# A transformer-layer kernel: the front of the program gets a fourth conditioning buffer, later state loads and a deeper token pipeline

## What is computed

```
sh1, sc1, g1, sh2, sc2, g2 = split(silu(cond) @ ada_w + ada_b, 6)    # cond: c_ctx and c, two rows
h = rms_norm(x, norm1_g) * (1 + sc1) + sh1                          # x_sample gets a position table first
z = h @ w_in                                                        # 2816 columns
y_rwkv, s_new = rwkv7_bidir(z_shift, z_g, s0, p)                    # s0 = state_rwkv for latent tokens
y_conv = conformer_conv(z_conv, p)                                  # 31 taps per channel
```

## Time and profile before

| | |
|---|---|
| time of the kernel before, median of 3 runs | 1143.97 us (1143.56 to 1144.54) |
| the profiled execution: span from first to last instruction | 1138.3 us |
| what lies around the span, against the median | 5.7 us |
| PE busy | 890.6 us (78%) |
| DVE busy | 550.1 us (48%) |
| ACT busy | 300.0 us (26%) |
| GpSimd (POOL) busy | 45.3 us (4%) |

### The profile page before, as it was taken

How to read it: one execution, slowest core, us unless ns; L and a number is a source line. 1 busy time by engine, 2 the same in 40 slices (tenths; PEclk the granted TensorE clock), 3 DMA queues, 4 the chain that set the end, 5 groups by cost and what they waited for, 6 DMA issues and landing times.

```text
span 1138.3 us, 17266 instructions
## 1 busy us (share of the span) xinstructions
PE 890.6 (78%) x6827; PEld 540.6 (47%) x6827; DVE 550.1 (48%) x1112; ACT 300.0 (26%) x522; POOL 45.3 (4%) x50
## 2 busy tenths in 40 slices
PE   1599988999988796967958959693298897997764
PEld 0366544666665674756746624343233242442321
DVE  1426999855357767677651534436611021111116
ACT  2241000150654645475212252101011010110102
POOL 0000000000000000000000000001101011110010
PEclk9989999999988587685765979795599898998987
DMA  9843354111200202001044078320499999997952
GB/s 316 266 192 130 134 215 186 61 56 29 20 2 10 21 1 30 2 11 21 4 81 163 4 238 318 145 93 37 157 419 421 420 420 410 419 420 293 417 204 118
DMA packets 75246, 196.50 MB, mean 173 GB/s; under 512 B 42885, under 2 KB 45311, under 8 KB 60959
## 3 DMA queue, kind: packets, MB, share of 16 engines
q1 hardware_dynamic: 66192, 174.19, 41.7%
q0 software_dynamic: 5472, 10.53, 2.5%
q10 hardware_dynamic: 3503, 10.68, 2.5%
HBM read 182.45 MB, written 21.31 MB: 179 GB/s over the span
## 4 chain that ended last, share of the span: by engine, by line
PE 42%; DVE 18%; DMA 13%; ACT 6%; issue 4%; SPq 2%; DVEq 0%; ACTq 0%; POOLq 0%
PE bank L2222 8%; DMA arena<-in_expert_w_up 7%; PE bank L539 5%; PE bank L1554 5%; DVE arena L969 4%; PE bank L2244 3%; PE bank L1222 2%; ACT arena L845 2%; PE bank L1279 1%; DMA arena<-winv 1%; DMA arena<-table_positions 1%; PE bank L1209 1%; PE bank L1282 1%; PE bank L1308 1%; DVE arena L1118 1%
## 5 line engine op out<-in xcount | busy, mean ns | idle before, releaser
L539 PE MATMUL bank<-arena 128*128 128x320 f32 x704 | 205.0, 446 | 2.1 <-ACT arena L389 2.1
L539 PEld LDWEIGHTS bank<-arena 128*128 128x128 f32 x704 | 133.6, 194 | 74.5 <-issue 25.3
L2222 PE MATMUL bank<-arena 128*64 128x512 f32 (+2 forms) x496 | 124.0, 665 | 22.2 <-DMA arena<-in_expert_w_up 21.3
L969 DVE SCALAR_TENSOR_TENSOR arena<-arena 128x655 f32<-128x655 f32 x116 | 104.7, 903 | 4.5
L2222 PEld LDWEIGHTS bank<-arena 128*64 128x64 f32 (+2 forms) x496 | 44.3, 152 | 100.2 <-issue 98.9
L2302 DVE TENSOR_TENSOR arena<-arena,bank 128x256 f32<-128x256 f32 x16 | 6.8, 422 | 141.7 <-ACT arena L2276 141.7
L1554 PE MATMUL bank<-arena 128*128 128x512 f32 x160 | 71.6, 605 | 0.0
L2244 PE MATMUL bank<-arena 128*64 128x512 f32 (+2 forms) x248 | 58.8, 599 | 9.4 <-DVE arena L2305 9.4
L1554 PEld LDWEIGHTS bank<-arena 128*128 128x128 f32 x160 | 30.7, 194 | 37.7 <-issue 37.7
L1308 PE MATMUL bank<-arena 64*64 64x64 f32 x320 | 32.5, 259 | 14.0 <-DVE arena L1136 14.0
L1308 PEld LDWEIGHTS bank<-arena 64*64 64x64 f32 x320 | 27.2, 167 | 26.4 <-DVE arena L1136 21.1
(11 more groups left out here) (352 smaller groups left out, 1300.3 us busy)
## 6 DMA issues: line engine op xcount, KB each, us to landing
arena<-in_expert_w_gate SPq DMA_DIRECT2D x33, 1024.0 KB, 16.7
arena<-in_expert_w_up SPq DMA_DIRECT2D x33, 1024.0 KB, 22.7
arena<-in_expert_w_down SPq DMA_DIRECT2D x33, 1024.0 KB, 22.2
arena<-in_ada_w SPq DMA_DIRECT2D x12, 2048.0 KB, 8.7
arena<-in_w_in SPq DMA_DIRECT2D x22, 512.0 KB, 3.8
arena<-expert_rows SPq DMA_DIRECT2D x10, 512.0 KB, 7.3
arena<-in_x_sample SPq DMA_DIRECT2D x8, 512.0 KB, 6.4
arena<-in_w_out SPq DMA_DIRECT2D x1, 4096.0 KB, 15.1
```

What stands on the lines that cost most here:

```text
L539: mm = nc.tensor.matmul(psum[4 + 2 * (n % 2) + half][:, 0:HALF], wring[:, n % NWIN, k], hT[:, k, half * HALF:(half + 1) * HALF], start=(k ...
L969: chain(nc.vector.scalar_tensor_tensor(acc, src, w, acc, ALU.mult, ALU.add))
L2222: mm = nc.tensor.matmul(psum[2 + n % 2][r, :], xeT[:, n % 2, c, r], gu[:, :, c, :], start=(c == 0), stop=(c == KD - 1))
```

## The change

All of it is in the first stage, except for renamed semaphores and one moved step.

- **A fourth buffer** `adaw3` for block 3, laid over `zlora`, `xlora` and `ysum`, which are free then. Block 3 has no wait any more and is issued between `w_in` tiles 0 and 1. Blocks 4 and up use the three old buffers; blocks 4, 5 and 6 wait for one summed block fewer than before. The three memsets of `zlora`'s padding move behind the wait for block 3's join.
- **States.** The eight loads leave SP's list and are issued by GpSimd, after a wait for the sum of block 3. `init.0` moves: on PE from between z.1.1 and z.1.2 to before `ada.5`, on DVE from behind `xl.0` to behind `tap.1.2`.
- **silu** moves on ACT from before the first square to between the copies of tiles 3 and 4.
- **Rows turned last.** PE's three transposes of the rows move behind those of the token tiles, and with them the DVE copies of `condP`, `par`, `convw` and `oneminus`. Block 1 now also waits for the last of these copies.
- **Token tiles two deep.** The position of tile i + 2 is added between the two halves of `normed(i)`, and ACT's root and copy are split off (`deviation`, `turned`), so that tile i's copy runs one step later.

```diff
+        adaw3 = view(zbase + 3 * PAIRS * ZT, KD * 512)
+        def ada_buffer(m):
+            if m == NADA:
+                return NADA, adaw3, 16
+            b = m if m < NADA else (m - NADA - 1) % NADA
+            return b, adaw[:, b], 16 * (1 + (m - 1) // NADA if m > NADA else 1)
 def ada_load(m):
-            if m >= NADA:
-                sp.wait_ge(s_adamm, m - NADA + 1)
+            if m > NADA:
+                sp.wait_ge(s_adamm, (m - NADA) if m <= 2 * NADA else m - NADA + 1)
 def sp_front():
             for m in range(NADA):
                 ada_load(m)
-            for a in range(8):
-                sp.dma_start(SL[0:64, a] ..., ins["state_rwkv"] ...).then_inc(s_sl, 16)
             win_tile(0)
+            ada_load(3)
             win_tile(1)
-            ada_load(3)
             win_tile(2)
 def pool_front():
+            nc.gpsimd.wait_ge(s_adamm, 4)
+            for a in range(8):
+                nc.gpsimd.dma_start(SL[0:64, a] ..., ins["state_rwkv"] ...).then_inc(s_sl, 16)
 def act_front():
-            act.wait_ge(s_rows, ROWS_ALL)
-            nc.scalar.activation(crow[0:16, :], crow[0:16, :], ACT.Silu).then_inc(s_silu, 1)
             square_sum(0)
             for i in range(TILES):
                 if i + 1 < TILES:
                     square_sum(i + 1)
-                turned(i)                      # square_sum held the root too
+                deviation(i)
+                if i:
+                    turned(i - 1)
+            act.wait_ge(s_rows, ROWS_ALL)
+            nc.scalar.activation(crow[0:16, :], crow[0:16, :], ACT.Silu).then_inc(s_silu, 1)
+            turned(TILES - 1)
 def dve_front():
+            def normed(i):
+                x = xt[:, i]
+                dve.wait_ge(s_xstat, i + 1)
+                ... variance ..., s_var, i + 1)
+                if i + 2 < TILES:
+                    position(i + 2)
+                dve.wait_ge(s_std, i + 1)
+                ... reciprocal, scale ..., s_xn, i + 1)
+            position(1)
+            for i in range(TILES):
+                normed(i)
+                if i:
+                    turned(i - 1)
+            turned(TILES - 1)
             dve.wait_ge(s_rowsT, 1)
             ... condP, par, convw, oneminus ...
-            for z in [zrkv[:, j, :] for j in range(12)] + [zlora]:
+            for z in [zrkv[:, j, :] for j in range(12)]:
             dve.wait_ge(s_modT, 4)
+            for c in (0, TP + 1, ZT - 1):
+                chain(nc.vector.memset(zlora[:, c:c + 1], 0.0))
 ORDER
-    pe:  ... z.1.1 init.0 z.1.2 ... z.6.0 ada.5 ...      dve: ... xl.0 init.0 join.4 ... tap.1.2 join.5 ...
+    pe:  ... z.1.1 z.1.2 ... z.6.0 init.0 ada.5 ...      dve: ... xl.0 join.4 ... tap.1.2 init.0 join.5 ...
```

More of the change, by code:

```diff
@@ L228, in build @@
         s_const, s_rows, s_lora = sem("constants_landed"), sem("rows_landed"), sem("lora_landed")
-        s_adaw = [sem(f"ada_block_landed{b}") for b in range(NADA)]
+        s_adaw = [sem(f"ada_block_landed{b}") for b in range(NADA + 1)]
         s_adab = [sem(f"ada_bias_landed{b}") for b in range(2)]
@@ L372, in square_sum, with deviation, turned @@
                                s_xstat, i + 1)
+            def deviation(i):
                 act.wait_ge(s_var, i + 1)
                 nc.scalar.activation(small[:, 8 + i:9 + i], small[:, i:i + 1], ACT.Sqrt).then_inc(s_std, 1)
+            def turned(i):
+                act.wait_ge(s_xT, i + 1)
+                chain.announce(nc.scalar.activation(
+                    hT[:, 0:4, i * P:(i + 1) * P], psum[4 + 2 * (i % 2)][:, :].rearrange("p (k t) -> p k t", t=P),
+                    ACT.Copy), s_hTa, i + 1)
             square_sum(0)
@@ L445, in dve_front @@
             chain(nc.vector.tensor_scalar(oneminus[:, 0:26], par[:, 0:26], -1.0, 1.0, ALU.mult, ALU.add))
[L446 to L468, removed]
-            for z in [zrkv[:, j, :] for j in range(12)] + [zlora]:
+            chain.announce(nc.vector.tensor_scalar(oneminus[:, 26:34], par[:, PAR["ka"]:PAR["ka"] + 8], -1.0, 1.0,
+                                                   ALU.mult, ALU.add), s_condT, 2)
+            for z in [zrkv[:, j, :] for j in range(12)]:
                 for c in (0, TP + 1, ZT - 1):
@@ L501, in ada_block @@
             pe = nc.tensor
-            pe.wait_ge(s_adaw[m % NADA], 16 * (m // NADA + 1))
+            b, w, landed = ada_buffer(m)
+            pe.wait_ge(s_adaw[b], landed)
             if m >= 2:
                 pe.wait_ge(s_adatmp, m - 1)
-            w = adaw[:, m % NADA].rearrange("p (k n) -> p k n", k=KD)
+            w = w.rearrange("p (k n) -> p k n", k=KD)
             for k in range(KD):
@@ L938, in act_mix @@
                     chain.announce(nc.scalar.activation(SL[0:64, 4:8], psum[7][0:64, :].rearrange("p (a b) -> p a b", b=P),
-                                                      ACT.Copy), s_finc, 1)
+                                                      ACT.Copy), s_s0, 2)
         def dve_pads(chain):
@@ L1346, in pe_mix @@
                                                  ST[:, 0, a, :], ident)
-                    mm.then_inc(s_fin, 1)
+                    mm.then_inc(s_slT, 1)
         EXPERT = 3 * 2048
```

42 lines of the change are left out of this document (28 added, 14 removed), and 8 rows, old and new, of the table ORDER.

## The result

| | before | after |
|---|---|---|
| median in the same series of runs | 1139.11 us (7 runs, 1135.93 to 1144.54) | 1131.19 us (7 runs, 1126.06 to 1132.75) |
| ratio of the two | | 0.9908 (95% interval 0.9880 to 0.9936) |
| profiled execution: span | 1138.3 us | 1127.2 us |
| profiled execution: its own time | not on record | 1128.92 us |
| first matmul of block 3 | 56.51 us | 45.18 us |

The change makes the kernel faster by 0.92%, some 10.5 us by the ratio (interval 0.64 to 1.20%). The ratio is worked out from all executions and is not the quotient of the two medians: that is 0.9930, or 7.9 us, and lies inside the interval. The ratio foretold (1133.3 / 1143.97) was 0.9907.

The account below looks back on a forecast made before the run. Bound: one DVE list waiting for z.2, behind block 3's load. z.0 -10.7, z.2 -0.6 and DVE +0.7 made -10.7 us: span 1138.3 to 1127.6, with 5.7 around it 1133.3; range 1130.5 to 1138.5.

Parts of the forecast that it names:

- Bound before: Up to 222 us: DVE's list can't begin before z.2 is summed, so the front is worth what it moves z.2.
- Block 3's landing: DMA queue in the front: block 3's load lands at 44.8 us, bounds 43.0 and 47.3.
- the states' price in the queue: DMA ahead of block 3: the eight state loads cost 2.5 us, which lets w_in tile 0 land at 39.8.
- The estimate of 0.85 us: States' DMA cost from descriptor cycles: 0.85 us; block 3 would land at 46.4, the gain 1.6 us less.
- Landing to z.0: Block 3's landing to z.0: 8.24 us as before, memsets 0.37, lower clock 0.6; z.0 at 54.0, 10.7 earlier.
- the middle way: Rival, front: PE stays at the lower clock or loads share the engines; 2 to 4 us less gain, 1136.5; chance 0.20.
- The level: Whole kernel: span 1127.6 plus the 5.7 us around it gives 1133.3, the same as 1143.97 - 10.7.
- Tokens: Front: tokens only have to stay ahead of block 3; shortened by over 10 us, they yield nothing beyond 44.8.
- Slower by the clock: Rival, z.0 to z.2: sparser PE work keeps the clock at 0.50 through them; 1149 us, chance 0.05.
- GpSimd in DVE's way: Rival, modulation of hT: GpSimd's eight issues lock out DVE; z.0 loses up to 4.4 us; 1135, chance 0.07.
- Nothing gained: Rival: block 3's load doesn't run ahead, or DVE's earlier start meets something fixed in time; 1143 us, chance 0.09.
- the likeliest case: Whole kernel: the forecast itself, chance 0.52, with its own bounds of 1130.8 to 1136.5 us.

Follow-up runs that it names:

- pe_kept_busy: Changed kernel with six added 128 x 512 matmuls on PE, behind the joins of blocks 0, 1 and 3; ratio to the kernel before 0.9895.
- front_trimmed: Changed kernel with block 3 issued ahead of w_in tile 0, low-rank weights loaded later and three added matmuls; 1120.07 us, ratio to before 0.9817.
- no_fourth_buffer: Changed kernel with block 3 back in block 0's buffer, loaded once block 0 is summed, behind w_in tile 1; ratio to the kernel before 0.9927.
- silu_first: Changed kernel with silu, the turning of the rows and their DVE copies ahead of the tokens again; ratio to the kernel before 0.9883.
- tiles_one_deep: Changed kernel with the token tiles one deep again, silu and rows still last; ratio to the kernel before 0.9877.
- lora_late: Changed kernel with the two low-rank weight loads on ScalarE's queue issued behind the modulation of hT; ratio to the kernel before 0.9863.
- init_back: Changed kernel with init.0 back between z.1.1 and z.1.2 on PE and ahead of join.4 on DVE; ratio to the kernel before 0.9907.

## Why the prediction was right and where it failed

**Bound before.** Right. z.2 sets the taps, and what the front gains reaches the end: the column "rest" is 1038.3 to 1043.6 in all fourteen profiles, while the taps start anywhere from 76.4 to 97.9. The 5.3 us by which it varies are half of what this change gains.

**Block 3's landing: 44.8 foretold, matmuls at 45.18.** Right, and so was the queue that I had named as what is late next. SP's issues were out at 14.7 us, long before the 27 allowed. One of its terms was too low: the states' price in the queue was taken as 2.5 us, which is the rate lost over 4 us and leaves out the states' own 0.26 MB, and undoing that part cost 4.0 to 4.6. The price of block 3 itself, 5.0 us, fits what came: block 2's matmuls began at 38.96, as it landed, and w_in tile 0 and block 3 behind it are 2.6 MB, 6.2 us at 422 GB/s, which is 45.2. The estimate of 0.85 us, worked out from the descriptor cycles in the Trainium skill (DMA: Bandwidth & Descriptors, "Why small descriptors are slow"), counts the states' own bytes and is further off.

**Landing to z.0: 9.21 foretold (8.24 + 0.37 + 0.6), 9.66 measured.** The three memsets took 0.35 (52.46 to 52.81) and block 3 went wholly to the lower clock: 3.64 instead of the 3.2 taken, near the upper bound of 3.86. z.0 at 54.84 instead of 54.0.

**z.0 to the taps.** A term was missing. The first z tile ran longer at the lower clock:

```profile
54.84:66.31 11.47, 11.47 (x33) 7.85 (x34) 1.81 (x7) 3.12 (x6) 0.00 (x0) 0.77 0.07 15
```

```profile
64.75:75.18 10.43, 10.43 (x33) 7.27 (x34) 1.69 (x7) 3.13 (x6) 0.00 (x0) 0.85 0.00 0
```

From its first matmul to ScalarE's first copy of it, the tile took 11.47 us at a mean clock of 0.77 (first row), against 10.43 at 0.85 before (second row). With the 0.64 of init.0 saved, z.2 should have been 10.6 earlier by z.0's shift and came 9.7 earlier. That is in part what the middle way (weight 0.20) had, and the runs show it can be avoided: the tile took 8.89 us in pe_kept_busy and in front_trimmed. At the first shift the gain was 8.9, where the sum had 10.7. Of the 1.8 us between them, 0.8 had gone by z.0 and another 0.85 between z.0 and the taps, where the first tile alone lost 1.0 and 0.2 came back behind it; init.0 on DVE, 0.7 in the sum, came to 0.8.

**The rest.** The profiled span fell by 11.1, not 8.9. The 2.2 us more come behind it. This chain element is the same work in both kernels, before and then after:

```profile
633.08 6.37 PE bank L1497 x16
```

```profile
625.05 4.68 PE bank L1524 x16
```

16 matmuls took 1.7 us less since the clock stood higher in that execution (1.00 against 0.73). The second profile of the changed kernel shows that this is not the change's doing, for there they take as long as before:

```profile
622.79 6.37 PE bank L1524 x16
```

The other 0.5 us were not traced.

That the span came out at 1127.2 where 1127.6 was foretold is luck: two errors that cancel, 1.8 us too much for the front and 2.2 us elsewhere.

**The level.** This step failed: "with the 5.7 us around it 1133.3, the same as 1143.97 - 10.7". I had set the 5.7 us between the median (1143.97) and the profiled span (1138.3) down as what lies around a span. In the thirteen later profiles it is 1.7 to 1.8 us (1128.92 less 1127.2, here), and so it is in every later execution of the kernel before. The other 4.0 us were the distance between the profiled execution and the median of three others.

That base was also high. The three executions behind 1143.97 lie at 1143.56 to 1144.54, and the four others of the same series at 1135.93 to 1139.11; the median of all seven is 1139.11, and 20 later ones span 14 us. So the range, 1130.5 to 1138.5, hung on a base 4.9 us too high and held no term for where it lies. The sum against the span, with 1.7 around it, gives 1129.3. The measured ratio times the median of before in its own series gives 0.9908 x 1139.11 = 1128.6. Both are below the low end. The plain median of the seven executions, 1131.19, lies 0.7 us inside, at the edge, and not near the 1133.3. Why executions of one kernel lie that far apart is open.

The relative forecast, 0.9907, did hold within the interval of 0.9880 to 0.9936. That it meets 0.9908 so closely is luck, since the terms of the front were 1.8 us too high.

**Tokens.** "The tokens only have to stay ahead" was right (no_fourth_buffer, silu_first, tiles_one_deep), and that the depth yields nothing beyond the DMA's 44.8 too. But I took being early as free. It is not: it opens a pause ahead of block 2 or block 3, and the clock falls.

**Rivals.** Slower by the clock: the lower level lasted to about 60 us and not through z.2. GpSimd in DVE's way: in the changed kernel only the last of the eight issues (49.16 to 54.11) lay over the modulations, which began at 53.44 and took 3.06 us, against 2.94 before. The better test is silu_first, where the issues ran from 46.92 to 51.93 and the modulations from 49.56: 2.95 us, with 2.4 us of issues over them. Refuted. The issues took 0.62 us each, not 0.55. The lock between GpSimd and DVE's fast modes that the Trainium skill (SBUF — State Buffer, "SBUF: two separate sides") describes didn't show; whether these instructions run in such a mode is not known. Nothing gained: refuted by the taps.

**Slips in the sums.** The 1149 of "slower" doesn't follow from the text: 16 us net above 1143.97 are 1160, half of that is 1152, and half of the 27 us lost gives 1147. The low bound of the likeliest case, 1130.8, is 1130.9 by its own terms. Neither touches the forecast.

## What to carry over

When a load is taken off a chain, ask what the queue would have let it do anyway: with this order of loads block 3 could not start before 44.6 us with its own buffer and before 46.5 without, and either end of the chain (tokens or load) alone gave about half. Being early has a price on TensorE: a step that arrives before its data may run at half the clock, and at the taps a few matmuls of filler (3.1 to 4.8 us) or a later, unbroken start (1.4 to 4.0 us) were worth as much as a part of the change. Build a forecast on spans or ratios of one series, and give the absolute level a term of its own for the scatter between executions.

## What was not expected of the hardware

- Two loads of 256 KB on a second queue (2 KB packets) took 2.8 to 3.3 us from a saturated DMA, where 0.52 MB take 1.2 us at 422 GB/s. Nothing but their place in time was changed, so whether packet size or the second queue does it is open. (This rests on one profile of lora_late against two.)
- The granted clock was 1.00 in a run of blocks without a pause (silu_first, tiles_one_deep). In all eight profiles with a pause of 2.0 to 6.3 us ahead of block 3 it was down to 0.50 when the block came or fell during it, and the same 16 matmuls took 2.60 to 3.64 us instead of 1.93. Shorter pauses didn't always do the same: behind 1.26 us ahead of block 2 (changed) the clock fell, behind 1.15 us (init_back) and 1.21 us (front_trimmed, ahead of block 3) it stayed. So the runs don't settle which pause brings the fall.
- Executions of one kernel in one series differ by up to 1.25% (1135.24 to 1149.44 us), and stretches at the lower clock that come and go are part of it: the same 16 matmuls took 4.68 and 6.37 us in two executions of the changed kernel.
